# Gate and up products that run on in their PSUM banks, with ScalarE copying the running sums out

## The reference, cut to what matters

```python
def swiglu(x, w_gate, w_up, w_down):
    return (jax.nn.silu(x @ w_gate) * (x @ w_up)) @ w_down

for layer in range(DEPTH):
    m = attn_conv_mixer(...) if layer % 2 == 0 else retention_mixer(...)
    x = layer_norm(DEEPNORM_ALPHA * x + m, *mix_norms[layer])
    x = layer_norm(DEEPNORM_ALPHA * x + swiglu(x, *ffn_params[layer]), *ffn_norms[layer])
```

## Time and profile before

| | |
|---|---|
| three runs | 1358.67, 1358.38, 1358.68 us, median 1358.67 |
| the profiled execution | 1357.12 us, of which 1355.3 us are its span |
| TensorE's granted clock over the span | 0.998 of full speed |
| busy over the span | PE 98%, DVE 72%, ACT 42%, POOL 14% |

### The profile page before, as it was taken

The page is one execution under the profiler, slowest core; times in us unless marked ns, Lnnn a source line. Parts: engine busy times, 40 slices in busy tenths (PEclk is TensorE's granted clock), DMA queues, the critical chain, the costliest instruction groups (busy, mean ns, idle before and its releaser), DMA issues.

```text
span 1355.3 us, 19504 instructions
## 1 busy us (share of the span) xinstructions
PE 1332.8 (98%) x7880; PEld 1180.4 (87%) x7880; DVE 978.8 (72%) x1211; ACT 564.0 (42%) x723; POOL 195.0 (14%) x161
## 2 busy tenths in 40 slices
PE   9999999999999999999999999989999999999997
PEld 8887878999999988898878878878899999998885
DVE  5999957998888533567877788763289988875336
ACT  3468834534434222334334444433144344343221
POOL 4011114111111000160313104000041111100001
PEclk9999999999999999999999999999999999999999
DMA  6210113233333432152123140242322333333221
GB/s 226 65 60 1 32 63 100 88 110 108 94 118 98 142 107 93 62 202 75 50 94 125 63 155 31 94 180 70 110 76 94 111 107 93 120 121 102 105 80 62
DMA packets 86352, 131.74 MB, mean 97 GB/s; under 512 B 2832, under 2 KB 61456, under 8 KB 86160
## 3 DMA queue, kind: packets, MB, share of 16 engines
q1 hardware_dynamic: 86288, 130.84, 29.2%
HBM read 126.63 MB, written 4.19 MB: 97 GB/s over the span
## 4 chain that ended last, share of the span: by engine, by line
PE 82%; DVE 11%; ACT 2%; DMA 2%; POOL 1%; issue 1%; DVEq 0%; SPq 0%; ACTq 0%; POOLq 0%
PE ps L1873 20%; PE ps L1875 20%; PE ps L1874 20%; PE ps L1951 19%; DVE w_lo L1718 2%; DMA raw<-in_l_w_in 2%; DVE acc L1262 2%; DVE w_lo L424 1%; POOL w_lo L424 1%; ACT w_hi L420 1%; PE ps L2128 1%; PE ps L1886 1%; DVE raw L1767 0%; DVE raw L1792 0%; DVE x_tok L1502 0%
## 5 line engine op out<-in xcount | busy, mean ns | idle before, releaser
L1873 PE MATMUL ps<-xT_hi,w_hi 128*128 128x256 f32 (+1 forms) x992 | 302.3, 305 | 0.5 <-POOL w_lo L424 0.5
L1875 PE MATMUL ps<-xT_hi,w_lo 128*128 128x256 f32 (+1 forms) x992 | 301.1, 304 | 0.0
L1874 PE MATMUL ps<-xT_lo,w_hi 128*128 128x256 f32 (+1 forms) x992 | 301.1, 304 | 0.0
L424 DVE TENSOR_TENSOR w_lo<-raw,w_hi 128x2048 fp32r<-128x2048 f32 x44 | 101.1, 2298 | 186.6 <-ACT w_hi L420 186.4
L1873 PEld LDWEIGHTS ps<-xT_hi,w_hi 128*128 128x128 f32 x992 | 189.5, 191 | 8.8 <-POOL w_lo L424 1.1
L1875 PEld LDWEIGHTS ps<-xT_hi,w_lo 128*128 128x128 f32 x992 | 189.5, 191 | 7.5
L1874 PEld LDWEIGHTS ps<-xT_lo,w_hi 128*128 128x128 f32 x992 | 189.6, 191 | 7.4
L420 ACT ACTIVATE w_hi<-raw 128x2048 fp32r<-128x2048 f32 x50 | 95.7, 1914 | 212.6 <-PE ps L1951 151.7
L988 ACT ACTIVATE sum_hi<-w_sum 128x1536 fp32r<-128x1536 f32 x38 | 56.5, 1488 | 183.4 <-PE ps L1875 182.7
L1873 PE MATMUL ps<-mix_hi,sum_hi 128*128 128x256 f32 x456 | 129.0, 283 | 0.0
L1874 PE MATMUL ps<-mix_lo,sum_hi 128*128 128x256 f32 x456 | 129.0, 283 | 0.0
(11 more groups left out here) (250 smaller groups left out, 2770.8 us busy)
## 6 DMA issues: line engine op xcount, KB each, us to landing
raw<-in_l_w_in SPq DMA_DIRECT2D x33, 1024.0 KB, 5.2
raw<-in_l_ffn_w_gate SPq DMA_DIRECT2D x22, 1024.0 KB, 5.3
raw<-in_l_ffn_w_up SPq DMA_DIRECT2D x22, 1024.0 KB, 5.3
raw<-in_l_ffn_w_down SPq DMA_DIRECT2D x22, 1024.0 KB, 4.9
raw<-in_l_w_out SPq DMA_DIRECT2D x12, 1024.0 KB, 5.1
x_tok<-in_x SPq DMA_DIRECT2D x4, 512.0 KB, 6.9
x_kept<-x_tok SPq DMA_DIRECT2D x1, 2048.0 KB, 9.1
x_tok<-x_kept SPq DMA_DIRECT2D x4, 512.0 KB, 7.4
```

Of the source, the lines that this page charges most:

```text
L424: eng.tensor_tensor(w_lo[ch.s][:], raw[ch.s][:], f32(w_hi[ch.s][:]), ALU.subtract)\
L1873: nc.tensor.matmul(dst, a[0], b[0], start=start, stop=False, skip_group_check=goes_on)
L1874: nc.tensor.matmul(dst, a[0], b[1], start=False, stop=False, skip_group_check=goes_on)
L1875: return nc.tensor.matmul(dst, a[1], b[0], start=False, stop=stop, skip_group_check=goes_on)
```

## The change: a chain of running sums, and who reads them

In a fast chunk TensorE now uses three places, x, y and z, each the first 256 columns of a bank. Four of the seven products run on in x: the first starts it, three more are added to it there. Two run on in z, one stands in y. Between them the running sum has to be read: x after its first and after its second product (ScalarE copies), z after its first (ScalarE copy), x after its third (VectorE adds it to a copy). TensorE may not write on until the reader is done, so it now waits at three places in a chunk. It waits for the first copy before its third product, for all three copies before the fifth, and for VectorE's first add before the seventh. VectorE does three adds of 256 columns for five (three of 256 columns and two of 512). Silu reads a quarter from x itself and becomes three instructions, and so does the multiplication in `fast_up`, whose last part reads the up chunk's x. `product_made` counts five steps a chunk for three. TensorE has the same 84 matmuls in a chunk, the second and third product having changed places.

```diff
-ADDS = 5
+ADDS = 3
+PRODUCTS = 5
+COPIES = 3
...
-                def product_copy(i, up, n):
-
-                    act.wait_ge(product_made, 3 * n + 1)
+                def first_copy(i, up, n):
+
+                    act.wait_ge(product_made, PRODUCTS * n + 1)
                     act.wait_ge(h_made, h0 + 2 * i)
                     nc.scalar.activation((gate32, up32)[up][:, 0, 0:256], ps[:, BANKS_OF[up][0], 0:256], ACT.Copy)\
                         .then_inc(product_copied, 1)
 
+                def other_copies(up, n):
+                    act.wait_ge(product_made, PRODUCTS * n + 2)
+                    nc.scalar.activation((gate32, up32)[up][:, 1, 256:512], ps[:, BANKS_OF[up][2], 0:256], ACT.Copy)\
+                        .then_inc(product_copied, 1)
+                    act.wait_ge(product_made, PRODUCTS * n + 3)
+                    nc.scalar.activation((gate32, up32)[up][:, 0, 256:512], ps[:, BANKS_OF[up][0], 0:256], ACT.Copy)\
+                        .then_inc(product_copied, 1)
+
                 def fast_gate(i, n):
                     act.wait_ge(tile_added, ADDS * n + ADDS)
-                    nc.scalar.activation(gate32[:], gate32[:], ACT.Silu).then_inc(gate_made, 2)
+                    act.wait_ge(chunk_used, c_ffn + 2 * i + 1)
+                    nc.scalar.activation(gate32[:, 1, 0:256], ps[:, BANKS_OF[0][0], 0:256], ACT.Silu)
+                    nc.scalar.activation(gate32[:, 0, :], gate32[:, 0, :], ACT.Silu)
+                    nc.scalar.activation(gate32[:, 1, 256:512], gate32[:, 1, 256:512], ACT.Silu).then_inc(gate_made, 2)
...
-                    product_copy(i, 0, n)
+                    first_copy(i, 0, n)
                     piece_hi(up, n + 1, 1)
+                    other_copies(0, n)
...
                         piece_hi(later, n + 2, 0)
-                        product_copy(i, 1, n + 1)
+                        first_copy(i, 1, n + 1)
                         piece_hi(later, n + 2, 1)
+                        other_copies(1, n + 1)
                         fast_gate(i, n)
...
-                product_copy(1, 1, third)
+                first_copy(1, 1, third)
+                other_copies(1, third)
                 piece_hi(Chunk(c_ffn + 4), fourth, 1)
...
-                def first_add(up, n):
-                    dst, (a, b, c, d) = (gate32, up32)[up], BANKS_OF[up]
-                    dve.wait_ge(product_made, 3 * n + 2)
-                    dve.wait_ge(product_copied, n + 1)
-                    nc.vector.tensor_tensor(dst[:, 0, 256:512], dst[:, 0, 0:256], ps[:, b, 0:256], ALU.add).then_inc(tile_added, 1)
-
-                def other_adds(ch, up, n):
-                    dst, (a, b, c, d) = (gate32, up32)[up], BANKS_OF[up]
-                    dve.wait_ge(product_made, 3 * n + 3)
-                    dve.wait_ge(tile_added, ADDS * n + 1)
-                    nc.vector.tensor_tensor(dst[:, 1, 256:512], dst[:, 0, 256:512], ps[:, a, 256:512], ALU.add).then_inc(tile_added, 1)
-                    dve.wait_ge(tile_added, ADDS * n + 2)
-                    nc.vector.tensor_tensor(dst[:, 0, :], dst[:, 0, :], ps[:, d, :], ALU.add).then_inc(tile_added, 1)
-                    dve.wait_ge(chunk_used, ch.c + 1)
-                    nc.vector.tensor_tensor(dst[:, 1, 0:256], dst[:, 1, 256:512], ps[:, c, 0:256], ALU.add).then_inc(tile_added, 1)
-                    dve.wait_ge(tile_added, ADDS * n + 4)
-                    nc.vector.tensor_tensor(dst[:, :, 256:512], dst[:, :, 256:512],
-                                            ps[:, c, 256:512].unsqueeze(1).broadcast_to([P, 2, 256]), ALU.add).then_inc(tile_added, 1)
+                def outer_adds(up, n):
+                    dst, (x, y, z, _) = (gate32, up32)[up], BANKS_OF[up]
+                    dve.wait_ge(product_made, PRODUCTS * n + 4)
+                    dve.wait_ge(product_copied, COPIES * n + 2)
+                    nc.vector.tensor_tensor(dst[:, 1, 256:512], dst[:, 1, 256:512], ps[:, x, 0:256], ALU.add).then_inc(tile_added, 1)
+                    nc.vector.tensor_tensor(dst[:, 0, 0:256], dst[:, 0, 0:256], ps[:, y, 0:256], ALU.add).then_inc(tile_added, 1)
+
+                def last_add(up, n):
+                    dst, (x, y, z, _) = (gate32, up32)[up], BANKS_OF[up]
+                    dve.wait_ge(product_made, PRODUCTS * n + 5)
+                    dve.wait_ge(product_copied, COPIES * n + 3)
+                    nc.vector.tensor_tensor(dst[:, 0, 256:512], dst[:, 0, 256:512], ps[:, z, 0:256], ALU.add).then_inc(tile_added, 1)
...
+                    nc.vector.tensor_tensor(rows(0), gate32[:, 0, :], up32[:, 0, :], ALU.mult)
+                    nc.vector.tensor_tensor(rows(1)[:, 256:512], gate32[:, 1, 256:512], up32[:, 1, 256:512], ALU.mult)
+                    dve.wait_ge(chunk_used, c_ffn + 2 * i + 2)
+                    nc.vector.tensor_tensor(rows(1)[:, 0:256], gate32[:, 1, 0:256], ps[:, BANKS_OF[1][0], 0:256], ALU.mult).then_inc(h_made, 2)
...
-                    for j in range(PIECES):
-                        piece_lo(up, n + 1, j)
-                    first_add(0, n)
+                    piece_lo(up, n + 1, 0)
+                    piece_lo(up, n + 1, 1)
                     if not last:
-                        weight_sums(later, n + 2)
-                    other_adds(gate, 0, n)
+                        weight_sums(later, n + 2, 0)
+                        weight_sums(later, n + 2, 1)
+                    outer_adds(0, n)
+                    if not last:
+                        weight_sums(later, n + 2, 2)
+                    last_add(0, n)
                     if last:
                         make_lo(dve, Chunk(c_down))
+                        outer_adds(1, n + 1)
                         rows_lo(0)
                     else:
-                        for j in range(PIECES):
-                            piece_lo(later, n + 2, j)
-                    first_add(1, n + 1)
-                    if not last:
-                        weight_sums(later_up, n + 3)
-                    other_adds(up, 1, n + 1)
+                        piece_lo(later, n + 2, 0)
+                        piece_lo(later, n + 2, 1)
+                        weight_sums(later_up, n + 3, 0)
+                        weight_sums(later_up, n + 3, 1)
+                        outer_adds(1, n + 1)
+                        weight_sums(later_up, n + 3, 2)
+                    last_add(1, n + 1)
                     fast_up(i, n + 1)
...
                 mix_lo_part(3)
                 piece_lo(Chunk(c_ffn + 4), fourth, 0)
+                outer_adds(1, third)
+                last_add(1, third)
                 piece_lo(Chunk(c_ffn + 4), fourth, 1)
-                first_add(1, third)
-                weight_sums(Chunk(c_ffn + 5), fourth + 1)
-                other_adds(Chunk(c_ffn + 3), 1, third)
+                for j in range(3):
+                    weight_sums(Chunk(c_ffn + 5), fourth + 1, j)
                 fast_up(1, third)
...
                         pe.wait_ge(h_made, NH * layer + 2)
                     else:
                         pe.wait_ge(tile_added, ADDS * (n - 1))
-                    fast_product(ps[:, b0, 0:256], a11, b11).then_inc(product_made, 1)
-                    fast_product(ps[:, b1, 0:256], s2, t2).then_inc(product_made, 1)
-                    fast_product(ps[:, b2, 256:512], s1, t1)
-                    fast_product(ps[:, b3, 0:256], a12, b21)
-                    fast_product(ps[:, b3, 256:512], s4, b22)
-                    pe.wait_ge(product_copied, n + 1)
-                    fast_product(ps[:, b0, 256:512], s3, t3).then_inc(product_made, 1)
+                        if up:
+                            pe.wait_ge(h_made, NH * layer + 2 * i)
+                        else:
+                            pe.wait_ge(gate_made, NH * layer + 2 * i)
+                    x, y, z = (ps[:, b, 0:256] for b in (b0, b1, b2))
+                    fast_product(x, a11, b11).then_inc(product_made, 1)
+                    fast_product(z, s1, t1).then_inc(product_made, 1)
+                    pe.wait_ge(product_copied, COPIES * n + 1)
+                    fast_product(x, s2, t2, start=False).then_inc(product_made, 1)
+                    fast_product(y, a12, b21)
+                    pe.wait_ge(product_copied, COPIES * n + 3)
+                    fast_product(x, s3, t3, start=False).then_inc(product_made, 1)
+                    fast_product(z, s4, b22, start=False).then_inc(product_made, 1)
                     if first and up:
                         pe.wait_ge(mix_lo_made, 4 * layer + 4)
-                    fast_product(ps[:, b2, 0:256], a22, t4).then_inc(chunk_used, 1)
+                    pe.wait_ge(tile_added, ADDS * n + 1)
+                    fast_product(x, a22, t4, start=False).then_inc(chunk_used, 1)
```

More of the change, by code:

```diff
@@ L2244, in swiglu, with fast_product @@
                 feature_tiles(ch, SIDE_A[0:2], lambda m: pe.wait_ge(gate_made, NH * layer + m + 1))
[L2246 removed]
+                def fast_product(dst, a, b, start=True):
```

(1 more changed line is left out.)

37 lines of the change are left out of this document (23 added, 14 removed).

## The result

The changed kernel takes 1369.47 us (median, 1368.19 to 1371.93, 4 runs) for 1358.53 us (1358.31 to 1358.68, 4 runs). The ratio is 1.0083, 95% interval 1.0065 to 1.0100: slower by 10.9 us, where 6.0 were forecast. The profiled execution took 1371.93 us, with a span of 1370.1 us and a mean granted clock of 0.993. It is the slowest of the four, so it shows more than the median holds.

A forecast was written before the change was run, and what follows sets the result against it. TensorE, full in the fast chunks, was taken to bound the kernel. Start stalls of 0.57 + 1.55 + 0.85 + 0.01 = 2.98 us a layer, 5.96 in two, gave a median of 1364.6 us, range 1360.3 to 1370.0.

The forecast's parts named there:

- What bounds the kernel: Whole fast-chunk stretch: TensorE is busy without gap, VectorE's adds are hidden under it, so removing VectorE work gains nothing.
- A chunk in the middle costs nothing: Middle fast chunks: each new wait is met 0.7 to 0.8 us before TensorE comes to it, so no cost.
- each new wait costs a little: Rival, all 38 fast chunks: waits cost although met, 6.8 us more at 0.06 each, 1371.5 us; 12%.
- no cover: Rival, all fast chunks: each return waits for its copy in full, 0.63 us, 72 us in all, 1430; 2%.
- the strict reading of the rule on rotating banks: All fast chunks: matmul groups should rotate through PSUM banks, so returning to x loses time in every chunk.
- The first stall, 0.57: First fast chunk of a layer, third product: TensorE waits 0.57 us for ScalarE's first copy, queued behind other work.
- The second, 1.55: Start of a layer's second fast chunk: TensorE waits 1.55 us for `w_lo`, queued behind the previous chunk's last add.
- The third, 0.85: Second fast chunk, third product: TensorE waits 0.85 us for ScalarE's copy, queued behind the next chunk's `sum_hi`.
- the clock falls: Rival: stalls let TensorE's clock fall to half speed for one chunk a layer, 20 us, 1385 us; 2%.
- The sum: Start of each layer's fast chunks: stalls of 0.57, 1.55, 0.85 and 0.01 us, 2.98 a layer, 5.96 in all.
- The range: Whole kernel: 8 in 10 from 1360.3 us, if the third stall and half the second are missing, to 1370.0.

The follow-up runs named there:

- b1: Kernel before, with the wait for the copy moved from sixth to third product of every fast chunk; 1367.15 us, ratio 1.0072.
- e1: Changed kernel, with the first fast chunk's first copy moved ahead of the next chunk's `sum_hi` on ScalarE; 1367.88 us, ratio 1.0081.
- e2: Changed kernel, with the second fast chunk's `w_lo` moved ahead of the first chunk's last add on VectorE; 1367.95 us, ratio 1.0077.
- e4: Changed kernel, with ScalarE's and VectorE's lists in the first fast chunk reordered nearer to a middle chunk's order; 1360.03 us, ratio 1.0013.
- c4: Kernel before, with one wait added: second fast chunk's third product waits for the low part of the next chunk's weights; 1373.39 us, ratio 1.0106.
- c3: Kernel before, with two waits added in the second fast chunk: its start for the last add, its third product for low weights; 1371.92 us, ratio 1.0107.
- e3: Changed kernel, with GpSimd's fourth sum for the third fast chunk held until pair 1's multiplication is done; 1368.06 us, ratio 1.0078.
- c1: Kernel before, with one wait added: the second fast chunk's third product waits for that chunk's copy; 1360.57 us, ratio 1.0022.

## Why the prediction was right in sign and short in size

**What bounds the kernel.** Right. TensorE's middle is full before and after, and 34 us less work on VectorE (forecast 40) bought nothing. The split multiplication took back more than I gave it, since in pairs 2 to 9 it now runs beside GpSimd's sum (1.07 to 1.48 us for 0.68).

**A chunk in the middle costs nothing.** Right, and most of the working held, to hundredths on ScalarE. From U2 to U10 every chunk takes 10.08 us, in both layers. The chunk that starts at 391.51 in the changed kernel:

```profile
393.15 0.38 ACT L1000 ACTIVATE up<-ps 128x256 f32<-128x256 f32 x1
...
396.04 0.38 ACT L1008 ACTIVATE up<-ps 128x256 f32<-128x256 f32 x1 [0.42 <-PE ps L1902]
```

```profile
399.24 0.42 DVE L1584 TENSOR_TENSOR up<-up,ps 128x256 f32<-128x256 f32 x1 [0.24 <-DVE w_sum L1562]
...
401.19 1.32 DVE L1598 TENSOR_TENSOR h<-gate,up 128x512 f32 x1 [0.22 <-DVE up L1591]
...
402.77 0.41 DVE L1601 TENSOR_TENSOR h<-gate,ps 128x256 f32 x1
```

```profile
391.51 0.28 PE L1900 MATMUL ps<-xT_hi,w_hi 128*128 128x256 f32 x1
...
401.60 0.28 PE L1900 MATMUL ps<-xT_hi,w_hi 128*128 128x256 f32 x1
```

Copy 1 ends at +2.02 (forecast 2.02), copy 3 at +4.91 (4.90), the first add at +8.15 (7.92) for 8.64, and the next chunk starts at 401.60, +10.09. One step was off here as at the start: `h_made` was forecast at about +10.7 and came at 402.77 + 0.41, +11.67, behind a multiplication that took 1.32 us beside GpSimd. That is the whole microsecond it had to spare, but no more: the copy that waits for it came at +11.76 for 11.7, and TensorE never waited for it. The rivals "each new wait costs a little" and "no cover" are out, and with them the strict reading of the rule on rotating banks (the Trainium skill, "Perfetto Trace Analysis", Optimizing Tensor Performance). Here a bank is written on after one other product without loss, as long as its reader is done within it. b1 is the case where the reader isn't.

**The first stall, 0.57.** Right: 0.57 in both layers, and e1 took it away.

**The second, 1.55.** Right: 1.44, and e2 took 1.1 of it away by the order of two calls. The missing 0.1 has two parts. The slow restart behind the first stall, which I didn't know of, let U1 end 0.1 later. And `w_lo` came no later for it, since the add ahead of it started 0.20 us behind the start of the seventh product (274.10 to 274.30) where I had taken 0.30.

**The third, 0.85: here the step failed.** The term was mis-sized because a duration in it was wrong. "The multiplication of pair 1, for which that copy waits too, ends at about 278.17 + 0.60 + 0.34 + 0.41 = 279.52": I put it in brackets as not deciding. It ended at 281.41: 0.6 us later because the whole stage began at 264.81 for 264.19, 1.1 by 1.50 for 0.41, and 0.2 by small gaps around the sums. Measured: 1.97 and 2.26, 2.5 us over the forecast in two layers. The durations came from rows of instructions beside which GpSimd stood still, and the trace of before did have the sign, at another place. There the same operation of 1024 columns takes 1.22 us when it starts ahead of GpSimd's sum and 2.20 when that sum is already running:

```profile
246.07 1.22 DVE L1618 TENSOR_TENSOR x_mix<-x_mix 128x1024 f32<-128x1024 f32 x1
247.32 2.20 DVE L1620 TENSOR_TENSOR x_mix<-x_mix 128x1024 f32<-128x1024 f32 x1
```

```profile
246.23 2.21 POOL L705 TENSOR_TENSOR raw<-raw,w_sum 128x512 f32<-128x512 f32 x1 [9.60 <-DVE w_sum L1544]
```

while every add from PSUM beside GpSimd's sum keeps its 0.41 or 0.69 us. Before, those adds are what lay there; the change put the multiplication there, in every pair, and only at the start did it matter. The Trainium skill, "SBUF — State Buffer", section SBUF: two separate sides, states it: a VectorE instruction with two SBUF inputs and a GpSimd instruction that reads SBUF take one pair of ports as a lock, and the later one waits for all of the earlier. The trace agrees: L1599 ended at 281.07, 0.28 us behind GpSimd's end at 280.79, and L1601, with an input from PSUM, took its 0.41.

**The rival "the clock falls".** I gave it 2% and 20 us, and both were wrong. The price was that of a whole chunk at half speed; a fall lasted 3.41 us and cost 1.5. The argument against it, that TensorE is busy for only 7.11 of 10 us in the earlier trace rows at a clock of 1.00, rested on one execution: the changed kernel's first profile, e1 to e4, b1 and c4 do show a fall just behind that very place, at 909 to 923. What is shown is that the stalls bring falls in the blocks: in four layers of four in c3 and c4, in none of the 14 with at most 2.0 us. What they cost the median, some 1.5 to 3 us of the 10.9, is the remainder and one profile each, not a measurement by itself.

**The sum.** Forecast 5.96. Stalls measured 8.25 (the first as forecast, the second 0.22 less in two layers, the third 2.5 more), restarts 0.6, falls behind them 1.5 to 3.0: 10.4 to 11.9 for 10.9.

**The range.** Its low end doesn't follow from its own words: without the third stall and half of the second the sum gives 1364.6 - 2 x (0.85 + 0.78) = 1361.3, not 1360.3. The measured time lies inside at either, near the upper end, and in part by luck: the 2.1 to 3.6 us of falls and restarts, which the sum doesn't have, were covered by a range made for other cases.

**Stays open.** Single runs of the kernel before spread from 1356.5 to 1359.9 us, the upper ones at a mean clock of 0.995 to 0.997. A fall in the retention stage would fit (seven profiles of other kernels have one), but no profile of the kernel before caught it.

## What to carry to other kernels

Before a chain of sums is let run on in its PSUM bank, ask for each return whether the reader is done within the products between, and ask it first at the start and end of the loop, where the lists are written by hand: here the middle cost nothing, and the order in two lists cost more than four fifths of the loss (e4). When an instruction moves in time, look which GpSimd instruction it now lies beside, and take its duration from a row with that neighbour, or its end from GpSimd's end (the list below). And look where the waiting work goes when a stall is removed: e3 took 1 us a layer out of one stall, and the delayed sum made two new ones as long; e2 kept 1 us a layer, since all that stood behind `w_lo` moved up with it. By the clock both look alike, 1.0078 and 1.0077 for 1.0083; only the traces tell them apart. e4 mended all three stalls and stands at 1.0013.

## What the runs showed that I had not expected

- VectorE's instructions with two SBUF inputs that start while GpSimd's sum of 512 columns runs: 0.41 to 1.50 us (256 columns), 0.68 to 1.49 (512), 1.76 to 2.69 (1536). What they add is no fixed price. They end a set time behind GpSimd's end, whenever they began: 0.28 us (256 columns, both layers), 0.55 (512, the 16 multiplications of pairs 2 to 9, and e4), 1.08 (1024, 247.32 above), 1.6 (1536, e3). So the 512 columns take 1.07 us where they start late in GpSimd's sum (320.80) and 1.48 where they start early (300.09). GpSimd's own sum went from 1.30 to 1.66 when it came second, and to 2.21 beside 1024 columns.
- The fall of TensorE's clock comes and goes between executions of the same kernel with stalls that agree to 0.01 us: 1.5 us for 3.41 us at 0.50.
- After a stall the second matmul comes 0.23 us behind the first for 0.12, 0.1 us a stall beside the wait itself.
- The kernel before, without any change, has single runs 3.4 us apart, more than the effect of e4 (1.8 us) or c1 (2.4 us). Those two needed 9 and 10 runs for an interval that clears 1.
